# A two-part model kernel on one core: smaller first transfers, gates in column groups, and adaLN weight chunks moved between TensorE, VectorE and the expert stage

## The chip, the cores and the metric

The kernel runs on one core of a Trainium2 chip. The metric is the device time of one execution in microseconds; the median of several runs is compared.

## What is computed

256 tokens of width 1024 in float32 go through two blocks. The first block has two layers, each a mixer, a layer norm and a mixture of experts; the second has two layers with adaLN modulation, two attentions and a feed-forward part. Shortened:

```python
def first_block(x, ...):
    h = x
    for i in range(2):
        mix = gla_mixer(h, ...) if i == 0 else mlstm_mixer(h, ...)
        h = layer_norm(ALPHA * h + mix, ln_g[i, 0], ln_b[i, 0])
        h = layer_norm(ALPHA * h + grouped_moe(h, ...), ln_g[i, 1], ln_b[i, 1])
    return h
# gla_mixer:   x @ w_in (3072 columns, and 16 of low rank for the decay), chunked linear attention, @ w_out
# mlstm_mixer: x @ w_in (4096 columns, and 8 gate columns), causal conv, chunked recurrence, @ w_out
# grouped_moe: 16 experts in 4 groups, best group, best 2 in it; y += gate * ((silu(t@w1) * (t@w3)) @ w2)
# second_block, per layer l: sh1, sc1, gt1, sh2, sc2, gt2 = split(silu(c) @ w_ada[l] + b_ada[l], 6)
#   h = rms(x) * (1 + sc1) + sh1; x += gt1 * (mixed attentions of h @ w_in[l]) @ w_out[l]
#   h = rms(x) * (1 + sc2) + sh2; x += gt2 * relu(h @ w_ff1[l])**2 @ w_ff2[l]
```

## The kernel before

**Stages.** They follow each other on all engines: mixer one (`gla_*`), its expert stage (`moe_*`, l=0), mixer two (`mlstm_*`), its expert stage (l=1), and the two layers of the second block (`dit_*`). Each engine runs its own program; semaphores join them.

**Weights.** All dense weights come in chunks of 1024 x 512 (2 MB) into a ring of four slots in SBUF. In the mixers slots 0 to 2 take the mixer's own chunks in turn, and slot 3 takes adaLN chunks of `w_ada`, 24 in all, that the second block needs much later: whichever engine has room multiplies them with silu(c) beforehand. In the expert stages the four ring slots and two more in the arena hold w1, w3 and w2 of a pair of experts; there are eight pairs. SyncE (SP) issues every load in a fixed order and waits before each until its slot is free (`slot_left`, L344, L404): a load that waits holds back all loads behind it.

**Precision.** A matmul in full precision is made of three products of a high and a low part (`three`, L612). ScalarE casts the high part of a quarter of a chunk (`mix_weight_hi`, L759), VectorE subtracts to get the low part in place (`mix_weight_lo`, L764), TensorE multiplies. Mixer one has 32 such steps n, mixer two 40; ScalarE and VectorE are up to three steps ahead (`LOOK`). Between the products each engine does at a fixed n what else the mixer needs; the tables and the `if n == ...` lines set that order by hand.

**adaLN chunks.** On TensorE a chunk is 16 products of 32 columns (`ada_rows`, L849, a table `*_ADA` says at which n), ScalarE copies (`ada_keep`) and eight small products fold the result (`ada_fold`, L864, table `*_FOLD`). On VectorE it is eight steps over 128x512 (`ada_step`, L711 and L714), summed over the partitions by four small products of TensorE (`ada_tensor`). Before, chunks 0 to 4 go to TensorE in mixer one and 5 to 9 in mixer two; VectorE takes later ones in the second block.

**Around the change.** At the start x is turned (`turn_x`, L792), split into `x_hi`, `x_lo` (L800, L805), the product with the 16 low-rank columns is made (24 products), and then n=0 follows. Mixer two begins with 48 products for the 8 gate columns. In the expert stages TensorE turns and routes (L507, L1354), multiplies constants into an unused bank (`keep_clock`, L785; one filling is one 128x512 product in full precision), waits for VectorE's choice of experts, computes places (L1361 to L1363), gathers tokens (L1399) and goes through the pairs (`up_pair` L1414, `down_pair` L1432). The second block's layers begin with such fillings and the turn of the modulated x (L2313). In mixer two VectorE's `weighed` (L2112) prepares what TensorE's state product (L1825) needs after n=24.

## Time and profile before

| | |
|---|---|
| median of 3 runs | 1673.93 us (1670.14 to 1676.1) |
| the profiled execution's own time | 1675.98 us |
| its span in the profile | 1674.2 us |
| granted TensorE clock, mean | 0.986 |
| TensorE busy | 1590.4 us, 95% |
| VectorE busy | 861.7 us, 51% |
| ScalarE busy | 650.4 us, 39% |
| bytes moved | 425.36 MB, mean 254 GB/s |

Times in the profile count from the span's start. PE is TensorE, DVE VectorE, ACT ScalarE, SP SyncE; "SPq" is a DMA issued by SP. A row of a timeline is: start, duration of the group, engine, line, operation, output<-input, partitions, elements, count, and in brackets the idle time before it with what ended it. L12 is line 12 of the kernel.

### The profile page before, as it was taken

To read this page: it belongs to the slowest core of one execution; us is meant where nothing else is said; L and a number is where in the kernel's file an instruction comes from. 1 tells how busy PE (TensorE), PEld (TensorE's weight loads), DVE (VectorE), ACT (ScalarE), POOL (GpSimd) and SP (SyncE) were. 2 spreads that over 40 slices of the span, in tenths; PEclk is the share of its full clock that TensorE was granted. 3 is DMA by queue.
4 is the path that set the end of the run, shared out by engine and by line. 5 is a ranking of instruction groups with operands and counts; after the bars stand their busy time and mean duration, and the time that the engine had idled before them with its cause. 6 is when DMAs were issued, how large, how long until landed. Compare 5 with 4: busy or idle time off the path is not lost.

```text
span 1674.2 us, 21147 instructions
## 1 busy us (share of the span) xinstructions
PE 1590.4 (95%) x8666; PEld 1089.5 (65%) x8666; DVE 861.7 (51%) x1316; ACT 650.4 (39%) x1056; POOL 41.4 (2%) x67
## 2 busy tenths in 40 slices
PE   5999899998999989999999999999999999999998
PEld 5766443442777654344337776689987777679997
DVE  2656112112766660212148964577777976566555
ACT  3434111111544421111136855544446676544443
POOL 2000000000000000000003000000002000000000
PEclk8999999999999999999999999999999999999999
DMA  9755899999676458999975424568764544537541
GB/s 318 273 187 207 349 427 425 421 426 307 197 222 170 186 214 336 423 426 425 424 276 160 167 101 176 199 253 301 263 249 167 176 153 175 191 113 300 201 152 26
DMA packets 114382, 425.36 MB, mean 254 GB/s; under 512 B 5020, under 2 KB 5368, under 8 KB 101352
## 3 DMA queue, kind: packets, MB, share of 16 engines
q1 hardware_dynamic: 110624, 416.81, 66.1%
q0 software_dynamic: 2304, 6.95, 1.5%
q8 instruction: 72, 1.18, 0.3%
q10 hardware_dynamic: 1352, 0.18, 0.1%
q14 instruction: 30, 0.25, 0.0%
HBM read 421.82 MB, written 1.05 MB: 253 GB/s over the span
## 4 chain that ended last, share of the span: by engine, by line
PE 74%; DVE 10%; ACT 6%; DVEq 4%; issue 2%; DMA 2%; ACTq 0%; SPq 0%
PE bank L612 35%; PE bank L1414 13%; PE bank L1432 7%; PE bank L1399 4%; PE bank L1444 3%; DVEq L713 2%; PE bank L2649 2%; DVE ring_r L2908 2%; DMA ring<-in_gla_w_in 1%; PE bank L785 1%; ACT parts_dit L560 1%; PE bank L849 1%; DVE parts_dit L563 1%; DVE ada_part L714 1%; PE bank L2651 1%
## 5 line engine op out<-in xcount | busy, mean ns | idle before, releaser
L1414 PE MATMUL bank<-ring,arena 128*64 128x512 f32 x1024 | 226.1, 594 | 1.5 <-ACT arena L1508 1.5
L612 PE MATMUL bank<-ring_r,x_hi 128*128 128x512 f32 x528 | 210.2, 398 | 0.0
L1696 DVE TENSOR_TENSOR arena<-arena,bank 128x512 f32<-128x512 f32 x16 | 16.7, 1044 | 363.0 <-PE bank L1414 363.0
L563 DVE TENSOR_TENSOR parts_dit<-ring,parts_dit 128x2048 fp32r<-128x2048 f32 x66 | 151.2, 2291 | 80.9 <-ACT parts_dit L560 80.8
L1414 PEld LDWEIGHTS bank<-ring,arena 128*64 128x64 f32 x1024 | 72.8, 137 | 139.7 <-issue 139.7
L612 PE MATMUL bank<-x_hi,parts_dit 128*128 128x256 f32 x896 | 163.1, 281 | 0.0
L612 PE MATMUL bank<-parts_dit,f_hi 128*128 128x512 f32 x512 | 160.5, 395 | 2.3 <-DVE parts_dit L563 1.4
L560 ACT CAST parts_dit<-ring 128x2048 fp32r<-128x2048 f32 x66 | 125.0, 1897 | 95.5 <-PE bank L612 95.5
L612 PEld LDWEIGHTS bank<-x_hi,parts_dit 128*128 128x128 f32 x896 | 138.5, 188 | 1.9 <-DVE parts_dit L563 1.7
L612 PE MATMUL bank<-in_whi,x_hi 128*128 128x512 f32 x304 | 125.4, 412 | 1.3 <-DVE x_lo L2350 1.3
L1432 PE MATMUL bank<-arena 128*64 128x512 f32 x512 | 115.1, 603 | 10.8 <-ACT arena L1534 10.8
L612 PE MATMUL bank<-x_lo,parts_dit 128*128 128x256 f32 x448 | 125.2, 280 | 0.0
L764 DVE TENSOR_TENSOR ring_r<-ring,mix_whi 128x1024 fp32r<-128x1024 f32 x72 | 86.8, 1221 | 68.0 <-ACT mix_whi L759 67.1
L612 PE MATMUL bank<-in_whi,x_lo 128*128 128x512 f32 x304 | 119.3, 392 | 0.0
L612 PEld LDWEIGHTS bank<-ring_r,x_hi 128*128 128x128 f32 x528 | 99.6, 189 | 19.4 <-issue 0.2
L612 PEld LDWEIGHTS bank<-parts_dit,f_hi 128*128 128x128 f32 x512 | 94.0, 188 | 26.3 <-DVE parts_dit L563 7.1
L2908 DVE TENSOR_TENSOR ring_r<-ring,in_whi 128x1024 fp32r<-128x1024 f32 x76 | 93.5, 1234 | 29.1 <-ACT in_whi L2733 27.7
L759 ACT CAST mix_whi<-ring 128x1024 fp32r<-128x1024 f32 x72 | 74.5, 1046 | 70.7 <-PE bank L612 58.2
L612 PE MATMUL bank<-parts_dit,f_lo 128*128 128x512 f32 x256 | 99.8, 390 | 0.0
L2733 ACT CAST in_whi<-ring 128x1024 fp32r<-128x1024 f32 x76 | 79.7, 1055 | 35.9 <-PE bank L612 35.8
L1432 PEld LDWEIGHTS bank<-arena 128*64 128x64 f32 x512 | 35.7, 138 | 79.9 <-issue 65.2
L612 PEld LDWEIGHTS bank<-x_lo,parts_dit 128*128 128x128 f32 x448 | 84.0, 188 | 0.2
(372 smaller groups left out, 2583.0 us busy)
## 6 DMA issues: line engine op xcount, KB each, us to landing
ring<-in_moe_w SPq DMA_DIRECT2D x64, 2048.0 KB, 12.5
ring<-in_w_ff SPq DMA_DIRECT2D x32, 2048.0 KB, 8.9
arena<-in_moe_w SPq DMA_DIRECT2D x28, 2048.0 KB, 13.0
ring<-in_w_ada SPq DMA_DIRECT2D x24, 2048.0 KB, 8.4
ring<-in_w_in SPq DMA_DIRECT2D x20, 2048.0 KB, 8.8
ring<-in_mlstm_w_in SPq DMA_DIRECT2D x8, 2048.0 KB, 13.8
ring<-in_gla_w_in SPq DMA_DIRECT2D x6, 2048.0 KB, 14.4
arena<-in_moe_w SPq DMA_DIRECT2D x8, 1024.0 KB, 10.7
```

Of the source, the lines that this page charges most:

```text
L560: return nc.scalar.copy(part_view(where, 0, h, form), half_of(ring[:, SLOT_OF[n], :], form, h))
L563: return nc.vector.tensor_tensor(part_view(where, 1, h, form), half_of(ring[:, SLOT_OF[n], :], form, h), part_view(where, 0, h, form).bitc ...
L612: last = pe.matmul(out, a[ka], b[kb], start=(first and i == 0), stop=(final and i == 2))
L713: dve.drain()
L759: nc.scalar.copy(quarter_hi(form, at), quarter_of(ring_slot(NUMBER[name]), form, q)).then_inc(in_hi, 1)
L764: nc.vector.tensor_tensor(quarter_of(ring_slot_r(NUMBER[name]), form, q), quarter_of(ring_slot(NUMBER[name]), form, q), quarter_hi(form, a ...
L1399: last = pe.matmul(ps[c // 4][:, (c % 4) * P:(c % 4 + 1) * P], x_sb[:, tt, c * P:(c + 1) * P], s_pick[:, tt, :], start=(tt == 0), stop=(tt ...
L1414: last = pe.matmul(bank[halves[h], :], s_x[:, p % 2, c, halves[h]], w[h][:, c, :], start=(c == 0), stop=(c == DC - 1))
L1432: last = pe.matmul(ps[6 + m][halves[h], :], s_hid[:, f, halves[h]], w[h][:, f, m * PSB:(m + 1) * PSB], start=(f == 0), stop=(f == 3))
L1444: last = pe.matmul(ps[2 * tt + m][:, :], s_gateT[:, p % 2, tt * P:(tt + 1) * P], s_y[:, m * PSB:(m + 1) * PSB], start=True, stop=True)
L2733: nc.scalar.copy(in_hi_of(l, n), ring_slot(NUMBER["in", l, j])[:, 2 * q:2 * q + 2, :]).then_inc(in_hi, 1)
L2908: v.tensor_tensor(ring_slot_r(NUMBER["in", l, j])[:, c, :], ring_slot(NUMBER["in", l, j])[:, c, :], in_hi_of(l, n).bitcast(F32), ALU.subtr ...
```

## The change

1. **Start.** The first chunk comes as two halves of 256 columns. The constants are laid out anew: 384 columns go right behind it, the other 2528 behind the last input chunk. The Pool queue holds its small loads (router, gates, gains) and the `rows` tables until chunk 3 of mixer one has landed. The low-rank product moves behind n=0.
2. **adaLN chunks.** Chunk 2 (mixer one) and chunks 6, 7, 8 (mixer two) go from TensorE to VectorE, in pieces at given n. Chunks 4 and 9 stay on TensorE but move into the expert stages: rows behind the router's products, fold behind the places.
3. **Fillings.** `keep_clock` in the expert stages 2 to 3 and 4 to 3; in the second block 10 to 6 for layer 0, and 2 new ones for layer 1.
4. **Mixer two.** The gates become 16 products in full precision in four column groups of 32, a copy by ScalarE and two products with a table of ones that sum the groups; copy, sums and the gate rows' activations come after n=0, VectorE's row chain after n=1. ScalarE's second head root (`head_root(1)`) moves behind the sigmoids of n=31, the second half turn from n=32 to 33.

TensorE in the expert stage of mixer two, from the router's sums to the gather (`chosen` is VectorE's choice, `c_act` silu(c)), before:

```order
L1354 MATMUL bank<-kst,arena 128x16 x2
L785 MATMUL bank<-kst 128x512 x4
L1361 MATMUL bank<-chosen,kst 128x32
L1362 MATMUL bank<-chosen,kst 128x16
L1363 MATMUL bank<-chosen,kst 128x32
L1399 MATMUL bank<-arena,x_sb 128x128 x16
```

and now:

```order
L1390 MATMUL bank<-kst,arena 128x16 x2
L875 MATMUL bank<-ring,c_act 32x512 x8
L811 MATMUL bank<-kst 128x512 x3
L1398 MATMUL bank<-chosen,kst 128x32
L1399 MATMUL bank<-chosen,kst 128x16
L1400 MATMUL bank<-chosen,kst 128x32
L890 MATMUL bank<-kst,ada_part 128x1 x4
L1440 MATMUL bank<-arena,x_sb 128x128 x16
```

Sixteen row products and the fold of an adaLN chunk now stand here, and one filling fewer.

SP at the beginning of the program (`kst` are the constants), before:

```order
L3143 DMA kst<-shape_constants 128x136
L3145 DMA x_sb<-in_x 128x1024 x2
L344 DMA ring<-in_gla_w_in 128x8x512 x2
L367 DMA kst<-shape_constants 128x2912
L344 DMA ring<-in_gla_w_in 128x8x512
L344 DMA ring<-in_w_ada 128x8x512
L344 DMA ring<-in_gla_w_in 128x8x512
```

and now, to the first load of an adaLN chunk:

```order
L3202 DMA kst<-shape_constants 128x136
L3204 DMA x_sb<-in_x 128x1024 x2
L348 DMA ring<-in_gla_w_in 128x8x256
L349 DMA ring<-in_gla_w_in 128x8x256
L375 DMA kst<-shape_constants 128x384
L352 DMA ring<-in_gla_w_in 128x8x512 x2
L352 DMA ring<-in_w_ada 128x8x512
```

The first chunk is in two parts, and 2528 columns of constants stand further behind.

VectorE in mixer two from n=22 on (L2098 and L2112 are `decays` and `weighed`, L2128 the state), before:

```order
L2098 SCALAR_TENSOR_TENSOR arena<-bank,arena,kst 128x128 x4
L2103 COPY arena<-bank 128x4
L2105 TENSOR_TENSOR arena<-arena,bank 128x256 x2
L2103 COPY arena<-bank 128x4
L2105 TENSOR_TENSOR arena<-arena,bank 128x256 x2
L764 TENSOR_TENSOR ring_r<-ring,mix_whi 128x1024
L2112 SCALAR_TENSOR_TENSOR arena<-bank,arena 128x512
L2171 TENSOR_TENSOR arena<-arena,rstd 128x2x2
L764 TENSOR_TENSOR ring_r<-ring,mix_whi 128x1024
L2128 COPY arena<-bank 128x257 x2
L2130 SCALAR_TENSOR_TENSOR arena<-arena,bank 128x257 x2
```

and now (L2156, L2170, L2186 are the same three, L723 and L726 the adaLN steps):

```order
L726 SCALAR_TENSOR_TENSOR ada_part<-ring,c_act,ada_part 128x512 x2
L2156 SCALAR_TENSOR_TENSOR arena<-bank,arena,kst 128x128 x4
L2161 COPY arena<-bank 128x4
L2163 TENSOR_TENSOR arena<-arena,bank 128x256 x2
L2161 COPY arena<-bank 128x4
L2163 TENSOR_TENSOR arena<-arena,bank 128x256 x2
L790 TENSOR_TENSOR ring_r<-ring,mix_whi 128x1024
L2170 SCALAR_TENSOR_TENSOR arena<-bank,arena 128x512
L2229 TENSOR_TENSOR arena<-arena,rstd 128x2x2
L790 TENSOR_TENSOR ring_r<-ring,mix_whi 128x1024
L726 SCALAR_TENSOR_TENSOR ada_part<-ring,c_act,ada_part 128x512 x3
L2186 COPY arena<-bank 128x257 x2
```

Two adaLN steps of chunk 8 stand ahead of `decays`, and three behind `weighed`.

```diff
@@ -66,11 +66,12 @@
-    ("ident", P), ("cols", 8), ("keep", P), ("addmask", P), ("dil", TT * 2 * T), ("cos_seq", TT * HD), ("sin_seq", TT * HD),
-    ("cos_ax", TT * HD), ("sin_ax", TT * HD), ("reset", T), ("pick", MH * P), ("before", PER * PER),
+    ("ident", P), ("cols", 8), ("keep", P), ("reset", T), ("addmask", P), ("dil", TT * 2 * T), ("cos_seq", TT * HD), ("sin_seq", TT * HD),
+    ("cos_ax", TT * HD), ("sin_ax", TT * HD), ("pick", MH * P), ("before", PER * PER),
...
+SECOND_N = FIRST_N + P + T
@@ -163,9 +164,9 @@
-        add(("gla_out", j), j == 0)
+        add(("gla_out", j), j == N_OUT - 1)
...
-        add(("ml_in", j), 2 <= p < 7)
+        add(("ml_in", j), p in (2, 3, 4, 6, 7))
@@ -214,7 +215,7 @@
-KEPT = {g: i for i, g in enumerate([*range(10), PAIR["out", 0, 1]])}
+KEPT = {g: i for i, g in enumerate([0, 1, 3, 4, 5, 9, PAIR["out", 0, 1]])}
@@ -341,6 +342,13 @@
+            if n == NUMBER["gla_in", 0]:
...
+                half = width // 2
+                sp.dma_start(slot_view(n, width)[:, 0:c, 0:half], src[:, :, 0:half]).then_inc(e_landed[0], 16)
+                sp.dma_start(slot_view(n, width)[:, 0:c, half:width], src[:, :, half:width]).then_inc(
+                    w_landed[SLOT_OF[n]], 16)
+                return
@@ -363,8 +371,11 @@
-                if j == 1:
-                    sp.dma_start(kst[:, FIRST_N:], const[:, FIRST_N:]).then_inc(const_landed, 16)
+                if j == 0:
+                    sp.dma_start(kst[:, FIRST_N:SECOND_N], const[:, FIRST_N:SECOND_N]).then_inc(const_landed, 16)
+                if j == N_GLA_IN - 1:
+                    sp.wait_ge(const_landed, 16)
+                    sp.dma_start(kst[:, SECOND_N:], const[:, SECOND_N:]).then_inc(const_landed, 16)
@@ -715,6 +727,15 @@
+        def mixer_ada(dve, work):
...
+            g, c0, c1 = work
+            if c0 == 0:
+                landed(dve, ada_chunk(g))
+                dve.wait_ge(ada_cols, g - 1)
+            for c in range(c0, c1):
+                ada_step(dve, g, c, ada_part[:, g % 2, :])
@@ -752,7 +773,12 @@
-            if q == 0:
+            if name == ("gla_in", 0):
+                if q == 0:
+                    act.wait_ge(e_landed[0], 16)
+                if q == QUARTERS // 2:
+                    landed(act, NUMBER[name])
+            elif q == 0:
@@ -893,8 +919,9 @@
-        GLA_ADA = {5: 0, 9: 1, 13: 2, 17: 3, 21: 4}
-        GLA_FOLD = {7: 0, 11: 1, 15: 2, 19: 3, 23: 4}
+        GLA_ADA = {5: 0, 9: 1, 19: 3}
+        GLA_FOLD = {7: 0, 11: 1, 18: 2, 21: 3}
+        GLA_WORK = {12: (2, 0, 1), 13: (2, 1, 4), 14: (2, 4, 5), 15: (2, 5, 6), 16: (2, 6, 8)}
@@ -913,12 +940,14 @@
-            pe.wait_ge(low_split, 1)
...
-            for c in range(DC):
-                last = three(pe, ps[3][0:RANK, 0:T], (wr_hi[:, c, :], wr_lo[:, c, :]), (xh[:, c, :], xl[:, c, :]),
-                             c == 0, c == DC - 1)
-            last.then_inc(gla_mm, 1)
...
+            def low_rank():
+                pe.wait_ge(low_split, 1)
+                for c in range(DC):
+                    last = three(pe, ps[3][0:RANK, 0:T], (wr_hi[:, c, :], wr_lo[:, c, :]), (xh[:, c, :], xl[:, c, :]),
+                                 c == 0, c == DC - 1)
+                last.then_inc(gla_mm, 1)
@@ -1015,6 +1044,7 @@
+                    low_rank()
@@ -1047,7 +1077,7 @@
-                    ada_fold(pe, GLA_FOLD[n], ps[3])
+                    (ada_fold if GLA_FOLD[n] in KEPT else ada_tensor)(pe, GLA_FOLD[n], ps[3])
@@ -1266,6 +1300,8 @@
+                if n in GLA_WORK:
+                    mixer_ada(dve, GLA_WORK[n])
@@ -1342,11 +1378,11 @@
-            pe.wait_ge(const_landed, 16)
+            pe.wait_ge(const_landed, 32)
...
-                    keep_clock(pe, ps[1], 2)
+                    keep_clock(pe, ps[1], 3)
@@ -1354,13 +1390,15 @@
-            keep_clock(pe, ps[2], 4)
+            ada_rows(pe, MOE_ADA[l], ps[3])
+            keep_clock(pe, ps[2], 3)
...
+            ada_fold(pe, MOE_ADA[l], ps[3])
@@ -1385,10 +1423,13 @@
+            pe.wait_ge(ada_read, MOE_ADA[l] + 1)
...
-
+            pe.wait_ge(m_added[l], 4 * NE + 1)
...
+        MOE_ADA = (4, 9)
@@ -1482,8 +1523,10 @@
+            ada_keep(act, MOE_ADA[l], ps[3])
...
+            ada_scalar(act, MOE_ADA[l], ps[3])
@@ -1728,8 +1772,11 @@
-        ML_ADA = {4: 5, 9: 6, 14: 7, 18: 8, 22: 9}
-        ML_FOLD = {6: 5, 11: 6, 16: 7, 20: 8, 24: 9}
+        ML_ADA = {4: 5}
+        ML_FOLD = {6: 5, 14: 6, 20: 7, 26: 8}
+        ML_WORK = {7: (6, 0, 3), 9: (6, 3, 5), 10: (6, 5, 6), 12: (6, 6, 8),
+                   14: (7, 0, 2), 16: (7, 2, 5), 17: (7, 5, 6), 18: (7, 6, 8),
+                   20: (8, 0, 2), 21: (8, 2, 3), 22: (8, 3, 5), 24: (8, 5, 8)}
@@ -1751,14 +1798,21 @@
-            pe.wait_ge(low_split, 2)
...
-            for a in range(2):
-                for c in range(DC):
-                    s = slice(a * MH, (a + 1) * MH)
-                    last = three(pe, ps[3][0:MH, a * T:(a + 1) * T], (wm_hi[:, c, s], wm_lo[:, c, s]), (xh[:, c, :], xl[:, c, :]),
-                                 c == 0, c == DC - 1)
+            for half in range(2):
+                for i, x in enumerate((xh, xl)):
+                    for a in range(4):
+                        c = 4 * half + a
+                        last = pe.matmul(ps[3][32 * a:32 * (a + 1), 0:T], w_mgate[:, c, :], x[:, c, :].bitcast(F32),
+                                         start=(half == 0 and i == 0), stop=(half == 1 and i == 1))
...
+            def sum_gates():
+                pe.wait_ge(ml["gates"], 1)
+                for a in range(2):
+                    last = pe.matmul(ps[3][0:MH, a * T:(a + 1) * T], k("sum4")[:, a * MH:(a + 1) * MH], m_sums, start=True,
+                                     stop=True)
+                last.then_inc(ml["mm"], 1)
@@ -1870,6 +1924,8 @@
+                if n == 0:
+                    sum_gates()
@@ -1931,21 +1987,23 @@
-            act.wait_ge(small_landed, SMALL)
-            nc.scalar.copy(wm_hi[:, :, :], w_mgate[:, :, :]).then_inc(low_hi, 1)
...
-            nc.scalar.activation(m_ig, ps[3][0:MH, 0:T], ACT.Identity, bias=b_mgate[:, 0:1])
-            nc.scalar.activation(m_fz, ps[3][0:MH, T:2 * T], ACT.Identity, bias=b_mgate[:, 1:2]).then_inc(ml["gates"], 1)
-            act.drain()
-            nc.scalar.activation(m_tmp, m_fz, ACT.Abs)
-            act.drain()
-            nc.scalar.activation(m_tmp, m_tmp, ACT.Exp, scale=-1.0)
-            act.drain()
-            nc.scalar.activation(m_tmp, m_tmp, ACT.Ln, bias=kcol(ONE, MH)).then_inc(ml["soft"], 1)
+            nc.scalar.copy(m_sums, ps[3][:, 0:T]).then_inc(ml["gates"], 1)
+            def gate_rows():
+                act.wait_ge(ml["mm"], 2)
+                act.wait_ge(small_landed, SMALL)
+                nc.scalar.activation(m_ig, ps[3][0:MH, 0:T], ACT.Identity, bias=b_mgate[:, 0:1])
+                nc.scalar.activation(m_fz, ps[3][0:MH, T:2 * T], ACT.Identity, bias=b_mgate[:, 1:2]).then_inc(ml["gates"], 1)
+                act.drain()
+                nc.scalar.activation(m_tmp, m_fz, ACT.Abs)
+                act.drain()
+                nc.scalar.activation(m_tmp, m_tmp, ACT.Exp, scale=-1.0)
+                act.drain()
+                nc.scalar.activation(m_tmp, m_tmp, ACT.Ln, bias=kcol(ONE, MH)).then_inc(ml["soft"], 1)
@@ -2042,21 +2100,21 @@
+                if n == 31:
+                    head_root(1)
...
-            dve.wait_ge(low_hi, 2)
...
-            dve.drain()
-            v.tensor_tensor(wm_lo[:, :, :], w_mgate[:, :, :], wm_hi[:, :, :].bitcast(F32), ALU.subtract).then_inc(low_split, 1)
-            for n in range(LOOK):
-                mix_weight_lo(dve, base + n, *ML_STEPS[n], "cols")
+            mix_weight_lo(dve, base, *ML_STEPS[0], "cols")
...
+            for n in range(1, LOOK):
+                mix_weight_lo(dve, base + n, *ML_STEPS[n], "cols")
@@ -2220,14 +2278,16 @@
-                if n == 33:
+                if n == 34:
...
-                if n == 0:
+                if n == 1:
...
+                if n in ML_WORK:
+                    mixer_ada(dve, ML_WORK[n])
@@ -2497,8 +2557,7 @@
-            if l == 0:
-                keep_clock(pe, ps[4], 10)
+            keep_clock(pe, ps[4] if l == 0 else ps[0], 6 if l == 0 else 2)
@@ -3155,6 +3214,7 @@
+            landed(pool, NUMBER["gla_in", 3])
```

## Rows read from the trace of the kernel before

**Rows 1.** The page: busy time of the engines, and shares of the last chain

```profile
PE 1590.4 (95%) x8666; PEld 1089.5 (65%) x8666; DVE 861.7 (51%) x1316; ACT 650.4 (39%) x1056; POOL 41.4 (2%) x67
...
PE 74%; DVE 10%; ACT 6%; DVEq 4%; issue 2%; DMA 2%; ACTq 0%; SPq 0%
```

**Rows 2.** Stretches: length, busy us of PE, PEld, DVE, ACT, POOL, PEclk, DMA share, GB/s

```profile
16.50:30.20 13.70, 4.89 (x23) 4.89 (x24) 4.63 (x4) 4.15 (x5) 0.00 (x0) 0.50 1.04 400
...
225.50:255.20 29.70, 29.02 (x144) 12.46 (x143) 5.22 (x15) 3.61 (x7) 0.00 (x0) 1.00 1.00 424
430.28:435.84 5.56, 5.56 (x48) 4.04 (x49) 0.00 (x0) 0.00 (x0) 0.00 (x0) 1.00 0.67 265
...
463.40:542.20 78.80, 78.80 (x514) 60.05 (x512) 50.23 (x104) 36.08 (x54) 0.00 (x0) 1.00 0.66 193
...
624.50:634.50 10.00, 9.23 (x52) 4.67 (x52) 1.87 (x8) 2.27 (x3) 0.00 (x0) 1.00 0.08 16
...
620.70:624.10 3.40, 3.40 (x19) 3.40 (x18) 0.00 (x0) 0.00 (x0) 0.00 (x0) 0.50 0.63 270
```

**Rows 3.** DMA, 5 to 12 us in 40 slices, and an issue: KB, us to landing

```profile
GB/s 410 421 363 386 413 354 387 375 395 401 433 337 293 179 120 85 85 123 117 111 64 23 26 0 0 0 12 26 47 56 73 76 79 94 91 164 190 220 281 393
...
kst<-shape_constants SPq DMA_DIRECT2D x1, 1456.0 KB, 28.9
```

**Rows 4.** Timeline of the start, TensorE and ScalarE

```profile
5.93 3.65 PE L792 MATMUL bank<-kst,x_sb 128*128 128x128 f32 x16 [5.93 <-DMA x_sb<-in_x]
...
22.96 2.94 ACT L759 CAST mix_whi<-ring 128x1024 fp32r<-128x1024 f32 x3 [12.56 <-DMA ring<-in_gla_w_in]
...
25.31 0.58 PE L612 MATMUL bank<-x_hi,mix_whi 128*128 128x256 f32 x1 [11.16 <-DVE ring_r L764]
...
30.43 0.24 PE L925 MATMUL bank<-kst,arena 92*128 92x92 f32 x1
```

**Rows 5.** Timeline: one instance of each piece that moves (TensorE, VectorE)

```profile
46.96 1.92 PE L849 MATMUL bank<-ring,c_act 128*32 128x512 f32 x16
...
54.58 0.95 PE L864 MATMUL bank<-kst,ada_part 128*128 128x1 f32 x8
...
157.62 0.91 PE L507 MATMUL bank<-arena,w_router 128*32 128x128 f32 x16 [1.26 <-ACT arena L495]
...
1096.59 2.41 DVE L714 SCALAR_TENSOR_TENSOR ada_part<-ring,c_act,ada_part 128x512 f32<-128x512 f32 x3
```

**Rows 6.** Timeline of the first expert stage's beginning, TensorE

```profile
163.43 5.30 PE L785 MATMUL bank<-kst 128*128 128x512 f32 x8
```

**Rows 7.** Mixer two: timeline of VectorE and TensorE; an issue of the page

```profile
537.71 0.68 DVE L2112 SCALAR_TENSOR_TENSOR arena<-bank,arena 128x512 f32<-128x512 f32 x1
...
542.15 1.14 PE L1825 MATMUL bank<-arena 64*128 64x257 f32 x8
...
579.09 0.50 PE L612 MATMUL bank<-mix_whi,x_hi 128*128 128x512 f32 x1 [2.37 <-ACT y_sb L2043]
...
ring<-in_w_ada SPq DMA_DIRECT2D x24, 2048.0 KB, 8.4
```

**Rows 8.** Timeline of the second expert stage's beginning, SP and TensorE

```profile
557.84 0.58 SPq L404 DMA_DIRECT2D ring<-in_moe_w  x1
...
600.13 3.14 SPq L404 DMA_DIRECT2D ring<-in_moe_w  x2
...
612.06 3.68 PE L785 MATMUL bank<-kst 128*128 128x512 f32 x8
...
617.60 0.41 PE L1361 MATMUL bank<-chosen,kst 128*128 128x32 f32 x2 [1.86 <-DVE chosen L1617]
...
626.13 4.08 PE L1414 MATMUL bank<-ring,arena 128*64 128x512 f32 x18 [0.77 <-ACT arena L1508]
```

**Rows 9.** Timeline of the second block's layers' beginnings, TensorE

```profile
865.21 10.55 PE L785 MATMUL bank<-kst 128*128 128x512 f32 x20 [3.38 <-issue]
...
1275.70 1.68 PE L2313 MATMUL bank<-kst,x_sb 128*128 128x128 f32 x8 [2.20 <-DVE x_sb L2436]
```

More of the change, by code:

```diff
@@ L184 @@
 assert len(PAIR) == DEPTH * N_ADA
-assert PAIR["ml_in", ML_ORDER[6]] == 9
+assert PAIR["ml_in", ML_ORDER[7]] == 9
 AFTER_MOE = [NUMBER["ml_in", 0], NUMBER["in", 0, 0]]
@@ L258, in build @@
         w_router = sb("w_router", [P, DC, 32])
-        w_mgate = sb("w_mgate", [P, DC, 2 * MH])
+        w_mgate = sb("w_mgate", [P, DC, 32])
         b_mgate = sb("b_mgate", [MH, 2])
@@ L384, in e_arrived @@
         def e_arrived(eng, k, count):
-            eng.wait_ge(e_landed[k], 16 * count)
+            eng.wait_ge(e_landed[k], 16 * (count + (1 if k == 0 else 0)))
         def moe_sync(sp, l):
@@ L451, in build @@
             (w_router[:, :, 0:NE], A["router_w"].rearrange("(p c) n -> p c n", p=P)),
-            (w_mgate[:, :, :], by_rows(A["mlstm_w_in"][0], PSB * N_ML_IN, 2 * MH)),
+            (w_mgate[:, :, 0:2 * MH], by_rows(A["mlstm_w_in"][0], PSB * N_ML_IN, 2 * MH)),
         ]
@@ L1068, in gla_scalar @@
                 turned_hi(act, 0, b, b, 4 + b)
-            act.wait_ge(w_rank_landed, 16)
-            nc.scalar.copy(wr_hi[:, :, :], w_rank[:, :, :]).then_inc(low_hi, 1)
             for n in range(LOOK):
                 mix_weight_hi(act, n, *GLA_STEPS[n], "cols")
+                if n == 0:
+                    act.wait_ge(w_rank_landed, 16)
+                    nc.scalar.copy(wr_hi[:, :, :], w_rank[:, :, :]).then_inc(low_hi, 1)
             act.wait_ge(gla_mm, 1)
@@ L1159, in gla_vector @@
             v.memset(w_router[:, :, NE:32], 0.0)
+            v.memset(w_mgate[:, :, 2 * MH:32], 0.0)
             for b in range(4):
                 turned_lo(dve, 0, b, b, 4 + b)
-            dve.wait_ge(low_hi, 1)
-            v.tensor_tensor(wr_lo[:, :, :], w_rank[:, :, :], wr_hi[:, :, :].bitcast(F32), ALU.subtract).then_inc(low_split, 1)
             for n in range(LOOK):
                 mix_weight_lo(dve, n, *GLA_STEPS[n], "cols")
+                if n == 0:
+                    dve.wait_ge(low_hi, 1)
+                    v.tensor_tensor(wr_lo[:, :, :], w_rank[:, :, :], wr_hi[:, :, :].bitcast(F32), ALU.subtract).then_inc(
+                        low_split, 1)
             def cumulate():
@@ L1563, in moe_vector @@
             v.memset(place[:, :, :], 0.0)
+            dve.wait_ge(const_landed, 32)
             dve.wait_ge(rt_exp, l + 1)
@@ L1717, in build @@
         m_ig, m_fz, m_tmp, m_bc, m_a, m_r, m_wk, m_wi = (area(42.5 + j, T, parts=MH) for j in range(8))
-        wm_hi, wm_lo = (area_r(n, a, [DC, 2 * MH]) for n, a in (("wm_hi", 51), ("wm_lo", 51.5)))
+        m_sums = area(54, T)
         m_pack = area(53, T, parts=MH)
@@ L1872, in mlstm_tensor @@
                 last.then_inc(in_used, 1)
+                if n == 0:
+                    sum_gates()
                 if n == 6:
@@ L1910, in mlstm_tensor @@
                     turn_half(0)
-                if n == 32:
+                if n == 33:
                     turn_half(1)
                 if n == 4:
-                    pe.wait_ge(ml["gates"], 1)
+                    pe.wait_ge(ml["gates"], 2)
                 if n in ML_ADA:
@@ L1917, in mlstm_tensor @@
                 if n in ML_FOLD:
-                    ada_fold(pe, ML_FOLD[n], ps[3])
+                    (ada_fold if ML_FOLD[n] in KEPT else ada_tensor)(pe, ML_FOLD[n], ps[3])
             pe.wait_ge(xt_split, 4 * SPLIT_TURNS[4] + 4)
@@ L1992, in mlstm_scalar @@
                 mix_weight_hi(act, base + ahead, *ML_STEPS[ahead], ml_form(ahead // QUARTERS))
+                if n == 0:
+                    gate_rows()
                 if n == 3:
@@ L2016, in mlstm_scalar @@
                         turned_hi(act, 4, i, b, 4 + i)
-                if n == 31:
-                    head_root(1)
-                if n == 33:
+                if n == 34:
                     for i, b in enumerate(HALVES[1]):
@@ L2222, in mlstm_vector @@
                     gated(1)
-                if n == 33:
+                if n == 34:
                     for i, b in enumerate(HALVES[1]):
@@ L2274, in build @@
         OWN, OWN_OUT, OWN_FF = 3, 1, 2
-        READ_ADA = [(10, N_ADA), (8, 10)]
+        READ_ADA = [(9, N_ADA), (8, 10)]
         ATT_STEPS = {11: (0, 0, 1), 12: (0, 1, 2), 13: (0, 2, 3), 15: (0, 3, 5), 17: (0, 5, 6), 19: (0, 6, 8)}
```

## The prediction

> **What bounds the kernel now.** The page comes first: TensorE is busy 95% of the span and the chain of work that ended last is 74% TensorE [rows 1]. So an instruction taken off TensorE is worth its own duration wherever TensorE runs without a gap, and the rest of the question is where it has gaps. The table of stretches [rows 2] shows both kinds. Inside the expert stage a pair of experts takes 29.70 us, TensorE busy 29.02, while the DMA runs at 424 GB/s with share 1.00: two limits at once. In mixer two, 463.4 to 542.2, TensorE has no gap, VectorE is busy 50.23 of 78.80, the DMA two thirds. The column PEclk shows where TensorE's clock was granted at half (0.50, that is 1.2 instead of 2.4 GHz): 16.5 to 30.2, and at 620.7 for 3.4 us, each time after TensorE had idled. 3.4 us of busy TensorE at half level cost 1.7 us. The timelines [rows 3 to 9] then give each place its price. The bound below which a measurement of this kernel cannot tell a change from none is 0.3%, 5 us.
>
> **The start: +11.2 us.** TensorE's first product of the mixer starts at 25.31, after 11.16 us of idling; behind it stands ScalarE's first cast, 12.56 us idle for the DMA of the first chunk [rows 4]. The bytes were not there because the queues nearly stood from about 7.5 to 10.5 us (slices 15 to 32 of the 40 that part 5 to 12 us; before them about 400 GB/s [rows 3]), while the small weights of the Pool queue were on the way; after that the `rows` tables and 1456 KB of constants, which took 28.9 us to land [rows 3], shared the rate with it. The change sends the first chunk as two halves, 1 MB each, directly behind x, and all of that small traffic later. x's first tile is there at 5.93 [rows 4] and its second, 512 KB behind it, by 6.8 to 7.2; 1 MB at about 390 GB/s is 2.7 us: the half lands at 9.6 to 10. From a landing to the first product it takes 25.31 − 22.96 = 2.35 us [rows 4], so the product starts at 12.0 to 12.4 (x's turn ends at 9.58 [rows 4], its casts are done before). n=0 is 24 products of 256 columns; 48 of them take 5.56 at full clock [rows 2], so 2.8: it ends at 15.3. The rank product, 24 such, 2.8 us, now stands behind it: 18.1. Before, n=0 ended at 30.43 [rows 4]: gain 12.3, less 1.7 if one stretch at half clock remains, which I expect about half the time: 11.2. Low end 0: the halves land no earlier. High end 12.5.
>
> **Mixer one: +3.7.** Chunks 2 and 4 lose their 16 row products, 1.92 us each in the row, 1.85 net of the overlap of ends [rows 5]: 3.7. Chunk 2's eight VectorE steps (2.41 us for three [rows 5], 0.8 each) fall where VectorE is idle over half the time. The fold of chunk 4, 0.8 [rows 5], goes too, but at n=24 TensorE then arrives as much earlier at a wait for ScalarE: nothing.
>
> **MoE0: +0.5.** As the order of the second expert stage shows (the first is the same), rows and three fillings stand where four fillings stood. The four took 5.30 us and the next product followed directly [rows 6]; three fillings (0.92 each at full clock: 3.68 for four [rows 8]) and the rows are 1.85 + 2.76 = 4.6. VectorE's choice ends the wait either way. A clock drop less may give 0.9; the fold costs 0.8: −0.7 to +1.2, taken 0.5.
>
> **Mixer two: +10.** The 48 gate products take 5.56 us [rows 2]. Now there are 16 full-precision ones in four column groups: the router's 16 of that kind, 128 columns wide, take 0.91 [rows 5]; twice as wide 1.82; the two products that sum the groups fill the array alone: at the groups' price 0.23, at four times that, which I take because the four groups no longer run side by side, 0.9. Gain 2.9. Chunks 6 to 9 lose their row products: 4 × 1.85 = 7.4. One fold fewer: 0.8. The wait of 2.37 us for ScalarE's sigmoid at n=31 [rows 7] goes, since the head's root stands behind it now: 2.4. Gross 13.5. Against it: 24 steps on VectorE, 24 × 0.82 = 19.7 us, onto 50 busy us [rows 2] of a stretch that becomes about 71. That is nearly full, so its short queues will be late. The place that I can price is the state product after n=24, 542.15; VectorE's weighing for it ended at 538.39 [rows 7], 3.8 us ahead. Rows 9 gone brings TensorE 1.9 nearer; five steps (n=20 to 22) ahead of it delay VectorE by 4.1: 2.2 us of waiting. The same kind costs about 0.5 at n=5 and 0.7 at the next state: 3.4 in all. Net 10.0. Ends: 13.5 (VectorE keeps pace) and 8 (VectorE also waits for chunks 7 and 8: it now releases their slot itself, a landing takes 8.4 us [rows 7], and it stands about 3 us at n=20).
>
> The Trainium skill, "VectorE: DVE Perf Modes", section "The DRAIN you can't avoid", says that an operation is followed by a drain of its duration less 266 ns; by that a step would be 0.75 + 0.48 = 1.23 us and the state's wait 2 us longer. The same section lets an operation that is not held start earlier, and the row bears that out: three steps in 2.41. A rival below.
>
> **MoE1: −5.0.** SP issues the loads in a fixed order and waits in it. Before: slot 3 at 557.84, then slot 1, then slots 2 and 0 at 600.13 [rows 8]. Chunk 9 now sits in slot 3 until its row products inside MoE1, behind the router's: 612.06 + 1.85 = 613.9. SP waits for it with slots 2 and 0 queued behind, though both are free at 600.13; slot 0 is half of the first pair. Then slots 3, 2, 0 come one after another at 424 GB/s, 4.94 us each: 615.3 + 14.8 = 630.1, against the first product of the pair at 626.13 [rows 8]. 4.0 to 4.5 late, an idle spell and the half clock behind it about 2, but the half-clock stretch at 620.7 [rows 2], costing 1.6 in the gather, follows the wait of 1.86 for `chosen` [rows 8], and three fillings and the rows cover that: −5.0. The DMA regains the rest: it stood at 16 GB/s from 624.5 to 634.5 [rows 2] and this room takes the two late arena loads. Ends: −3 and −14 (every late microsecond of 600 to 614 stays, because a pair has only 29.70 − 29.67 spare of the DMA, 12.58 MB at 424 GB/s).
>
> The Trainium skill, "DMA: Bandwidth & Descriptors", section "Specifications", names about 358 GB/s as the share of one core; by it three chunks take 17.6 instead of 14.8 us and this term would be −7.8. This trace disagrees with 424 over 29.7 us [rows 2], so the sum keeps to it.
>
> **The last two layers: +3.9.** Layer 0 runs ten fillings, 10.55 us, and the turn stands behind them [rows 9]. Six are gone by 872.0; VectorE's second tile is the next limit at about 872.5: +3.2 (2.7 to 3.4). In layer 1 two fillings lie inside the 2.20 us wait at 1275.70 [rows 9] and may spare a half-clock stretch behind it, worth 1.7 like the one at 620.7, or nothing: 0.7.
>
> **Sum.** 11.2 + 3.7 + 0.5 + 10.0 − 5.0 + 3.9 = 24.3. The profiled execution took 1675.98: 1651.7. The median of the runs is 2.05 lower; so 1650.
>
> **Rivals.**
> (A) VectorE keeps pace and MoE1 costs only 3: +3.5 and +2, up to 8 with a start of 12.5: 1644. For: 19.7 us fit in 28.5 idle. Against: queues are late locally, not on average.
> (B) The loads of MoE1 stay late for the stage, 14 instead of 5: 1659. For: the DMA's share of 1.00. Against: the slots wait about 10 us between landing and use there.
> (C) The first half does not land early, because x's own bytes or the split into packets of half the length take the rate: 1661. For: only that no row shows such a load; against: 400 GB/s before 8 us [rows 3].
> (D) Steps on VectorE cost 1.23: mixer two gains 7 to 8: 1653.
> (E) The other side. New short waits of TensorE in mixer two, n=5 to 26, drop its clock to half again and again. Each drop in the trace followed an idle spell; there is none now in that stretch [rows 2], and the change puts VectorE's lateness there. At half clock a microsecond of work takes two, so once more than 24.3 × 2 = 49 us of the 71 run at 1.2 GHz the kernel is slower; all of it would give 1650 + 35 = 1685. Against: at 620.7 the full clock was back after 3.4 us of busy TensorE, and the waits that I price are single ones of 0.5 to 2.2 us.
>
> **Chances.** Forecast 0.58; A 0.17; B 0.09; C 0.05; D 0.05; B and C together, or half the sum for reasons not seen, 0.03 (about 1670, no difference); E 0.03. Faster by over 0.3%: 0.94; within 0.3%: 0.03; slower: 0.03. The range goes from A with its best ends, 1640, to C, 1661.
>
> **What would show it.** First product near 12.2 and n=0 over by 15.5; the start wrong if ScalarE's first cast still waits for the DMA beyond 12. Mixer two: VectorE over 65 us busy between the same steps, TensorE's waits for weighing near 2 us. MoE1: TensorE idle 4 to 5 us ahead of the first pair, waiting for the load of slot 0; if it does not wait, that step is wrong. Layer 0: 6 fillings, then the turn at 3 us less. The forecast fails as a whole if new waits of TensorE for VectorE in mixer two sum to more than 7 us.

## The result and the profile after

The changed kernel took 1660.02 us (1659.31 to 1661.92, four runs), the kernel before 1673.06 beside it (1670.14 to 1676.1): ratio 0.9924, 95% interval 0.9903 to 0.9944. That is 13.0 us less, inside the range, 10 above the forecast of 1650, and only 1 below the range's upper end. That end was set by rival C, which did not happen: that the time still fell inside is partly luck. The profiled execution after took 1659.87, the one before 1675.98: between the two traces lie 16.1, and 3 of them are only that the profiled execution before lay high among its runs. The sum of 24.3 is to be held against 16.1.

"Before" and "after" stand below for the two kernels' traces. The waits of TensorE show most of it at a glance (us in total, times, longest). The view of after:

```profile
PE bank L811 <- issue: 10.0, 3, 5.1
...
PE bank L1455 <- DMA ring<-in_moe_w: 5.4, 1, 5.4
...
PE bank L624 <- DVE ring_r L790: 3.8, 2, 3.4
...
PE bank L624 <- ACT arena L2093: 1.7, 1, 1.7
...
PE bank L1879 <- DVE arena L2170: 0.8, 1, 0.8
...
PE bank L875 <- DMA ring<-in_w_ada: 0.7, 1, 0.7
```

The wait of 11.16 for the first chunk's low part [rows 4] is now 3.40, the sigmoid's 2.37 [rows 7] is gone, and one of 5.40 for expert weights is new.

The timeline of TensorE in after, at the points that answer to [rows 4, 7, 8, 9]:

```profile
12.95 0.55 PE L624 MATMUL bank<-x_hi,mix_whi 128*128 128x256 f32 x1 [3.40 <-DVE ring_r L790]
...
20.88 0.24 PE L954 MATMUL bank<-kst,arena 92*128 92x92 f32 x1
...
417.97 0.64 PE L1806 MATMUL bank<-x_hi,w_mgate 128*32 128x256 f32 x8 [1.88 <-DVE x_lo L831]
...
519.49 0.50 PE L624 MATMUL bank<-mix_whi,x_hi 128*128 128x512 f32 x1 [1.74 <-ACT arena L2093]
...
521.97 1.14 PE L1879 MATMUL bank<-arena 64*128 64x257 f32 x8 [0.82 <-DVE arena L2170]
...
593.14 0.41 PE L1398 MATMUL bank<-chosen,kst 128*128 128x32 f32 x2 [0.78 <-DVE chosen L1661]
...
607.75 4.79 PE L1455 MATMUL bank<-ring,arena 128*64 128x512 f32 x12 [5.40 <-DMA ring<-in_moe_w]
...
848.80 5.42 PE L811 MATMUL bank<-kst 128*128 128x512 f32 x12 [3.39 <-issue]
...
1059.19 1.94 PE L2373 MATMUL bank<-kst,x_sb 128*128 128x128 f32 x8 [2.83 <-DVE x_sb L2496]
```

Subtracting the start of the same instruction in the two traces gives a ledger. The forecast beside it is the prediction's term.

| up to | before | after | gained so far | in this stretch | forecast |
|---|---|---|---|---|---|
| first work behind n=0 and the rank product | 30.43 | 20.88 | 9.55 | 9.6 | 11.2 |
| router, first expert stage | 157.62 | 144.90 | 12.72 | 3.2 | 3.7 |
| last pair, first expert stage | 402.62 | 388.43 | 14.19 | 1.5 | 0.5 |
| gates, mixer two | 430.28 | 417.97 | 12.31 | −1.9 | none |
| router, second expert stage | 607.13 | 582.66 | 24.47 | 12.2 | 10.0 |
| first pair, second expert stage | 626.13 | 607.75 | 18.38 | −6.1 | −5.0 with the next |
| last pair, second expert stage | 851.11 | 834.69 | 16.42 | −2.0 | |
| layer 0, first mixer product | 880.56 | 861.08 | 19.48 | 3.1 | 3.2 |
| end | 1674.2 | 1658.1 | 16.1 | −3.4 | 0.7 |

Where the clock was at half in after (length, busy us of PE, PEld, DVE, ACT, POOL, PEclk, DMA share, GB/s):

```profile
12.95:18.06 5.11, 5.11 (x24) 5.09 (x25) 2.42 (x3) 1.04 (x1) 0.00 (x0) 1.00 1.05 386
147.80:154.60 6.80, 6.71 (x41) 2.53 (x40) 4.84 (x16) 1.23 (x4) 2.31 (x1) 0.51 0.69 280
404.00:410.80 6.80, 6.56 (x8) 2.74 (x9) 5.16 (x7) 2.51 (x3) 1.06 (x2) 0.53 1.00 204
594.90:601.70 6.80, 5.94 (x28) 5.94 (x29) 1.37 (x8) 0.00 (x0) 0.00 (x0) 0.51 1.00 425
605.00:611.60 6.60, 3.85 (x10) 1.24 (x12) 0.00 (x0) 0.00 (x0) 0.00 (x0) 0.50 1.00 427
943.10:946.50 3.40, 3.40 (x12) 2.78 (x11) 1.31 (x2) 1.19 (x3) 0.00 (x0) 0.53 0.02 5
1059.20:1062.50 3.30, 3.30 (x12) 2.98 (x13) 0.00 (x0) 2.12 (x7) 0.00 (x0) 0.52 0.00 0
```

In the second expert stage two stretches stand where one of 3.40 stood [rows 2]. The last two rows are new, and the same work ran at full clock before. A stretch of 3.4 us at 857.6 is left out here; before has one at the same work. In the first row the clock's column says 1.00, yet 24 products took 5.11 us, 0.21 each, as at half; in this trace the column does not show that stretch at the very start, the spacing of the products does (a second trace of the same kernel has it in the column too, from 13.2 on).

### The profile page after: what moved, and what is told of

Its sections match the earlier page's. It is cut to its first block, busy times and chain, and to the rows that moved or that the text cites. A ratio compares the mean times of both kernels' runs of the same rounds, so it can differ in the third digit from the quotient of the medians.

```text
span 1658.1 us, 21045 instructions
## 1 busy us (share of the span) xinstructions
PE 1581.1 (95%) x8586; PEld 1085.3 (65%) x8586; DVE 885.5 (53%) x1348; ACT 647.0 (39%) x1051; POOL 40.4 (2%) x67
## 4 chain that ended last, share of the span: by engine, by line
PE 72%; DVE 12%; ACT 6%; DVEq 5%; DMA 4%; issue 2%; ACTq 0%; SPq 0%
PE bank L624 34%; PE bank L1455 14%; PE bank L1473 7%; PE bank L1440 3%; PE bank L1485 3%; DVEq L725 2%; DVE ring_r L2967 2%; PE bank L2708 2%; DMA ring<-in_w_ada 1%; DVE ada_part L726 1%; DMA ring<-in_moe_w 1%; ACT parts_dit L572 1%; DVE parts_dit L575 1%; PE bank L811 1%; DMA ring<-in_w_ff 1%
## 6 DMA issues: line engine op xcount, KB each, us to landing
ring<-in_moe_w SPq DMA_DIRECT2D x64, 2048.0 KB, 13.3
```

## The experiments

Each ran beside the kernel before; ratios are to it. The changed kernel's ratio is 0.9924.

### The order of SP's loads in the second expert stage

```diff
-by_release = sorted(range(SLOTS), key=lambda k: last[k]) + list(range(SLOTS, ROLES))
+by_release = [k for k in sorted(range(SLOTS), key=lambda k: last[k]) if k != SLOTS - 1] + list(range(SLOTS - 1, ROLES))
```

> The changed kernel with one difference: in the second expert stage SP asks for slots 1, 2 and 0 first and for slot 3 (the one that chunk 9 holds) after them. Theory (SP's order made TensorE wait 5.40 us ahead of the first pair, and the idle spell brought a second half-clock stretch worth about 2): no wait for a DMA of the expert weights at the first pair, it starts about 5.4 us earlier in the stage, 1653 to 1654 in all against 1660. Rival (the DMA's rate is the bound at this place, whatever the order): the wait only moves to slot 3 a few products later, and the time stays at 1658 to 1660.

1655.17 us (1651.44 to 1657.29), ratio 0.9874 (0.9846 to 0.9902). In after, the view of SP's waits has this row:

```profile
SPq L416 <- PE bank L875: 33.8, 1, 33.8
```

SP stood 33.8 us until the row products of chunk 9 had freed slot 3, with loads for free slots queued behind. With the order turned, TensorE at the same place:

```profile
595.89 5.46 PE L1440 MATMUL bank<-arena,x_sb 128*128 128x128 f32 x32 [0.90 <-DVE arena L1592]
602.12 4.08 PE L1455 MATMUL bank<-ring,arena 128*64 128x512 f32 x18 [0.77 <-ACT arena L1551]
```

No wait for weights is left. Counted from the router's first product, the same instructions come 0.7 us earlier than in after in the gather, 5.8 at the first pair and 7.5 four products later: 6.8 us from this place alone, 5.4 of waiting and the rest the half-clock stretch behind it. The medians differ by less, 4.9 us, and the time lies 1 to 2 above the theory's 1653 to 1654. The mechanism holds; the rival, that the DMA's rate is the bound there whatever the order, falls.

### The Pool queue's wait alone

```diff
 pool.dma_start(w_up, A["gla_w_gate_up"][0]).then_inc(w_up_landed, 16)
+landed(pool, NUMBER["gla_in", 3])
```

> The kernel before with one line of the change: the Pool queue holds its small loads and the rows tables until chunk 3 of mixer one has landed. The first chunk stays whole, the constants stay where they were. Theory (the small Pool loads stalled the queues and the rows tables shared them): the first product of the mixer starts at about 15 instead of 25.31, so this line alone brings 9 to 10 of the start's gain, 1663 to 1665. Rival (halving the chunk is what brings it): the first product stays later than 20, the time within 4 us of before.

1668.76 us (1664.39 to 1671.41), ratio 0.9949 (0.9923 to 0.9976). ScalarE's first cast, in this kernel:

```profile
13.03 2.94 ACT L759 CAST mix_whi<-ring 128x1024 fp32r<-128x1024 f32 x3 [2.64 <-DMA ring<-in_gla_w_in]
```

It was 22.96 [rows 4]. n=0 was over at 18.50, 11.9 us earlier than before, and 2.4 earlier than in the changed kernel. So this line brings all of the start's gain and more, at that point. Of the 11.9 only 7.6 were left by 85 us, when TensorE had waited for the second adaLN chunk and run a stretch at half clock:

```profile
68.79 2.06 PE L849 MATMUL bank<-ring,c_act 128*32 128x512 f32 x12 [2.64 <-DMA ring<-in_w_ada]
```

In the changed kernel TensorE waits 0.7 for such a chunk. The theory on the cause of the stall holds; its 9 to 10 us at the end do not, 4.6 are left between the spans and 6.0 between the medians.

### The first chunk whole

```diff
-sp.dma_start(slot_view(n, width)[:, 0:c, 0:half], src[:, :, 0:half]).then_inc(e_landed[0], 16)
-sp.dma_start(slot_view(n, width)[:, 0:c, half:width], src[:, :, half:width]).then_inc(
-    w_landed[SLOT_OF[n]], 16)
-return
```

> The changed kernel with the first chunk in one piece, everything else as changed. Theory: the chunk lands 2.7 to 3 us later than its first half did, the first product of the mixer at 15.7 instead of 12.95, 2.7 to 3 us slower, 1662 to 1663. Rival (the later traffic sets the pace of mixer one, not the first product): the same time as the changed kernel, 1659 to 1661.

1658.67 us (1656.86 to 1661.27), ratio 0.9906 (0.9877 to 0.9935). The first product came 2.2 us later than in after, at 15.17, and at 52 us the lag was 1.5 (2.1 against the second trace of the changed kernel, below). The medians do not show it: 1.5 us faster than the changed kernel beside it, within what the runs differ. So the theory's 2.7 to 3 us at the end failed, and the rival's "the same time" held: halving the chunk is worth 1.5 to 2.1 us at 52 us by the traces, and nothing that the medians can tell.

### The low-rank product ahead of n=0 again

```diff
+low_rank()
...
                 if n == 0:
-                    low_rank()
                     turn_params()
```

(and the casts of its weights ahead of the first steps on ScalarE and VectorE)

> The changed kernel with the low-rank product back ahead of n=0 (on ScalarE, VectorE and TensorE), everything else as changed. In the changed kernel TensorE idles 3.40 us ahead of n=0 and n=0 then takes 5.1 us, its products 0.21 apart; with the Pool wait alone the low-rank product filled that idle time, n=0 took 2.8 us and was over at 18.5 instead of 18.1 with the rank product already done. Theory (the reordering gave away the cover): rank product 11.2 to 14.0, n=0 over at 16.8 to 17.2 instead of 20.88 for both, 3.5 to 4 us faster, 1656 to 1657. Rival (n=0 runs at half pace in any order, because the engine has been idle before it): over at 19 to 19.3, 1.7 faster at most.

1656.61 us (1655.56 to 1658.66), ratio 0.9901 (0.9873 to 0.9929); the changed kernel beside it 1660.13 (below). TensorE:

```profile
11.01 0.28 PE L624 MATMUL bank<-x_hi,wr_hi 128*16 128x256 f32 x1 [1.69 <-DVE wr_lo L1195]
...
16.65 0.25 PE L956 MATMUL bank<-kst,arena 92*128 92x92 f32 x1
```

Both products, low-rank and n=0, are done at 16.65 instead of 20.88; the idle time of 3.40 is filled. The time is 3.5 us less by the medians, and by the spans 4.2 less than after and 5.1 less than the changed kernel's second trace. The reordering in the change cost that much.

### The changed kernel again

> The changed kernel itself once more, on the chip that runs the others of this call. Theory: 1659 to 1662, the waits of its first profile at the same places. What may differ is where the stretches at half clock and the waits behind code loads fall (so far 1.48 us in mixer two's fillings).

1660.13 us (1658.58 to 1661.06), ratio 0.9916 (0.9888 to 0.9944). Between its two traces the lag of the same instruction swings from −3.1 to +3.1 us: the half-clock stretch at the first expert stage's beginning lay elsewhere, and the entry to mixer two came 2.4 us later in the second. So a term under some 2 us cannot be read off the end of two traces.

The second trace also shows what sets the first pair of the second expert stage. Here the gather ran at full clock:

```profile
598.83 3.84 PE L1440 MATMUL bank<-arena,x_sb 128*128 128x128 f32 x32 [0.90 <-DVE arena L1592]
610.59 1.98 PE L1455 MATMUL bank<-ring,arena 128*64 128x512 f32 x4 [7.92 <-DMA ring<-in_moe_w]
```

The wait grew from 5.40 to 7.92, and the pair began 24.9 us after the router's first product, against 25.1 in after. The landing sets this time; a faster or slower gather ahead of it changes nothing.

### Both edits

> The changed kernel with both edits: SP's order in the second expert stage with slot 3 last, and the low-rank product ahead of n=0. Theory: the gains add, 5 to 7 and 3.5 to 4, 1649 to 1652. Rival: the start's gain is taken back by waits for chunks within mixer one, 1653 to 1655.

> The kernel with both edits (slot 3 last in SP's order, low-rank product ahead of n=0) once more, as the base of the two that follow. Theory: 1648 to 1651.

SP's order and the low-rank product first: 1649.27 us (1643.91 to 1654.18), ratio 0.9855 (0.9816 to 0.9893), and again 1651.07 (1649.47 to 1652.28), 0.9851 (0.9832 to 0.9871). The gains add: this beats both kernels.

### Fewer fillings at the beginning of mixer two

```diff
-            keep_clock(pe, ps[4], 6)
+            keep_clock(pe, ps[4], 2)
```

> The changed kernel with 2 instead of 6 fillings at the beginning of mixer two. The trace of the changed kernel has x ready on VectorE at 408.08, but the turn starts at 414.18, behind 12 passes of fillings of which 7 ran at half clock, and a gap of 1.48 us. Theory (the fillings are the bound there): the turn starts at 408 to 410, 4 to 5 us earlier, 1655 to 1656. Rival (without the fillings the clock stays at half through the turn and the gates, or VectorE's splitting is the bound): 1658 to 1661.

1659.93 us (1657.08 to 1664.38), ratio 0.9893 (0.9864 to 0.9922). By the median nothing was gained; the ratio is a little lower than the changed kernel's, but the intervals overlap. TensorE in this kernel (a filling is two records, so "x4" is two fillings):

```profile
406.61 3.78 PE L811 MATMUL bank<-kst 128*128 128x512 f32 x4 [6.75 <-issue]
410.18 1.70 PE L818 MATMUL bank<-kst,x_sb 128*128 128x128 f32 x7
416.56 2.08 PE L818 MATMUL bank<-kst,x_sb 128*128 128x128 f32 x9 [4.68 <-issue]
```

The turn did start four us earlier, and then stopped in the middle for 4.68 us, waiting for nothing that a semaphore shows. A packet of the instruction queue falls in that gap (DMA view, 413.5 to 415.5):

```profile
q8 instruction: 1, 0.02, 2.9%
```

It carries 16 KB, starts at 414.16, and TensorE goes on at 416.56, 2.4 us later. The same pair stands in each trace: packet and restart at 401.81 and 404.24, 411.49 and 413.75 in after, 417.19 and 419.62 in before. The second gap also keeps its place in TensorE's program: it lies ahead of the 1972nd product (counted in the trace) in ten of the twelve traces of changed kernels, be that a filling (after) or a part of the turn (here); with the whole first chunk it is the 1973rd, and one trace has no such gap. I read the packet as a load of TensorE's code, and the fillings as work that hides it; no run changed the load itself, so this stays a reading. Neither theory nor rival had the gap. The rival was right in its other half: the clock was at half again from 415.2 to 425.5, through the turn's end and the gates, which took 3.6 us instead of 1.9, and its 1658 to 1661 holds.

### Chunks 6 to 8 back on TensorE

```diff
-        ML_ADA = {4: 5}
-        ML_FOLD = {6: 5, 14: 6, 20: 7, 26: 8}
+        ML_ADA = {4: 5, 9: 6, 14: 7, 20: 8}
+        ML_FOLD = {6: 5, 11: 6, 16: 7, 22: 8}
```

(and `ML_WORK` empty)

> The changed kernel with chunks 6, 7 and 8 back on TensorE in mixer two (rows at n=9, 14, 20, folds at n=11, 16, 22), and no adaLN steps of VectorE there. Theory: TensorE gets 3 x 1.85 = 5.6 us more work and loses the waits that VectorE's fuller list caused (0.44, 1.74, 0.82 and 0.20 us): about 2.4 us slower than the changed kernel, 1662 to 1663. Rival (VectorE's list costs nothing net, the waits stay): 5 to 6 slower, 1665 to 1666. Rival (moving them was no gain): 1660 or less.

> The kernel with both edits, and chunks 6, 7, 8 back on TensorE in mixer two. The first kernel of this kind was 2.0 us slower inside mixer two plus one stretch at half clock, but stalls at the beginning of mixer two blurred its whole time. Theory: 2 to 2.5 us slower than the base at the end of mixer two by the two traces, 1651 to 1653 in all. Rival: 5.6 or more slower.

On the changed kernel: 1665.38 us (1658.58 to 1672.34, nine runs), ratio 0.9938 (0.9915 to 0.996). Its runs lie far apart. The trace shows 2.7 us lost between the first expert stage's last pair and mixer two's gates, where the second gap named "issue" is 4.14 instead of 1.48. On the kernel with both edits: 1655.30 us (1651.59 to 1657.33), ratio 0.9874 (0.9851 to 0.9898), 4.2 slower than its base, where 2 to 2.5 had been expected. VectorE and TensorE between 420 and 520 us, in the changed kernel and in the first of these two:

```profile
420.00:520.00 100.00, 97.82 (x668) 82.61 (x669) 82.43 (x162) 52.62 (x87) 0.00 (x0) 1.00 0.58 171
```

```profile
420.00:520.00 100.00, 97.90 (x711) 78.52 (x710) 67.97 (x130) 50.95 (x84) 0.00 (x0) 1.00 0.67 192
```

The steps put 14 us more on VectorE in this window and save TensorE its row products; the waits that they cause (1.74 and 0.82 in after) are gone here, while the 0.44 at n=5 stays (0.45): that one is not theirs. From the gates to the router the two kernels take 4.5 and 5.1 us longer than after and the base; 1.7 of each is a half-clock stretch near 520 us. Moving the three chunks is worth about 4 us, between my 2.4 and the rival's 5.6 or more.

### Row products in place of the first fillings

```diff
-                    keep_clock(pe, ps[1], 3)
+                    ada_rows(pe, MOE_ADA[l], ps[1])
...
-            ada_rows(pe, MOE_ADA[l], ps[3])
-            keep_clock(pe, ps[2], 3)
+            keep_clock(pe, ps[2], 4)
```

> The kernel with both edits, and in both expert stages the row products of chunks 4 and 9 take the place of the first three fillings, behind the first tile's turn, with four fillings instead of three at the second place. Theory: there they cover a wait for ScalarE and VectorE, as the fillings did; behind the router's products they stand ahead of fillings and in a half-clock stretch. Slot 3 is free about 6 us earlier. Per stage 0.5 to 1.5 us faster: 1647 to 1648. Rival (VectorE's choice is what ends that place, the order of TensorE's work ahead of it changes nothing): same as the base.

1651.86 us (1649.29 to 1652.47), ratio 0.9855 (0.9835 to 0.9875): as its base, 1651.07. The rival held.

### The fillings of the last two layers as before

```diff
-            keep_clock(pe, ps[4] if l == 0 else ps[0], 6 if l == 0 else 2)
+            if l == 0:
+                keep_clock(pe, ps[4], 10)
```

> The changed kernel with the fillings of the second block as before: ten ahead of layer 0's turn, none in layer 1. Theory (the fillings stood on the path in layer 0): the turn of layer 0 and the first product of its mixer 3 us later than in the changed kernel; what of it remains at the end depends on where the half-clock stretches at 943 and 1059 fall: 1660 to 1663. Rival (the shorter filling is what caused those two stretches, which the kernel before did not have): they are gone, and the time is the same or lower, 1659 to 1660.

1662.39 us (1659.14 to 1665.47), ratio 0.992 (0.9895 to 0.9944). Against after, layer 0's first mixer product lost 3.1 us at this place, and the half-clock stretches near 946 and 1062 were there again. So they do not come from the shorter filling; what brings them stays open. They were missing in before and in the kernel with the whole chunk, which has the changed kernel's fillings, and the changed kernel's second trace has only the later one. In layer 1, where this kernel has no fillings, the wait of 2.20 is back, and yet no half-clock stretch follows it. So the two fillings there are not shown to be what spares the stretch that before has at 1276.

## Why the prediction was right and where it was wrong

**Direction and range held**, and four of the six terms lie within 2 us. The sum was 8.2 us too high against the trace; the last two layers (4.2 us), the second expert stage (3.1) and the start (1.6) make it up, and the first expert stage gave 1.0 more than forecast.

**The start, 11.2 forecast, 9.6 measured.** The cause was right: the small loads of the Pool queue held up the first chunk, and their wait, together with that of the `rows` tables behind them, brings n=0 to 18.50; the two are not separated. The landing was nearly right (first product at 12.95, forecast 12.0 to 12.4). The term has a slip: 12.3 less half of 1.7 is 11.45, not 11.2. The stretch at half clock, to which I gave a chance of one half, came, and cost 2.3 instead of 1.7: all but the last two of n=0's products ran at that pace, 5.1 us as in before. I took the moved low-rank product as neutral; it had filled the idle time, and putting it back gave 3.5 us. That part of the change works against the rest.

**Mixer one and first expert stage, 3.7 and 0.5 forecast, 3.2 and 1.5 measured.** At n=24 the wait for ScalarE grew from 0.44 to 1.34, as the term has it; a new wait of 0.69 for a weight chunk at 52 us is the rest. Up to the first pair the expert stage lost 0.2, inside my ends; 1.7 came from a half-clock stretch at 197 us that before had and after has not. That gain is luck.

**Mixer two, 10.0 forecast, 10.3 measured** from the first expert stage's last pair to the router, but of other parts. Inside the mixer 12.2 were gained. The gates' term holds: 1.9 us and 1.0 for the two sums, forecast 1.8 and 0.9, against 5.7 before; no run tests it or the sigmoid's wait alone. Waits of 0.44, 1.74, 0.82 and 0.20, 3.2 in all, stand against my 3.4, and the 0.44 is not due to the steps. VectorE was busy 63.0 us over the mixer's same products where before it was 50.2; I had asked for over 65. At the entry 1.9 were lost, a step that the sum did not have: nearly all of the half-clock stretch of 6.8 us fell on the fillings, where half of before's fell into its idle gap, and a second gap of 1.48 came on top. The 12.2 hold 1.7 from a half-clock stretch at 580 that is gone: together they nearly cancel, so 10.3 meets 10.0 by some luck.

By the drain rule of the Trainium skill, "VectorE: DVE Perf Modes", section "The DRAIN you can't avoid", the wait ahead of the state product would have been the 2.2 us of the sum and 2 more. It was 0.82, and with the 1.74 just ahead of it 2.6; three steps in a row took 2.40 us in after's mixer two, as the row of before has it (2.41). The trace does not bear that rival out for these steps.

**Second expert stage, −5.0 forecast, −8.1 measured.** The mechanism was right: SP waits for slot 3, TensorE for the pair, 5.40 us. The row products ended as forecast, and the 2 us of half clock behind the pair came. Two steps failed in size. The first pair began 6.1 us late, where I had 4.0 to 4.5: I gave the three loads 16.2 us from the end of the row products, and they landed 8.0, 13.3 and 18.2 us after it; the first took longer, the others came 5 us apart as forecast. And I took 1.6 back because fillings and rows would cover the clock's drop in the gather. They did not cover it (the clock fell at 594.7, between a wait of 0.78 and one of 0.90, for 6.8 us instead of 3.4), but that was no loss either: the pair waits for a landing, so nothing could be had back ahead of it. The −7.8 that the prediction works out from a slower DMA comes nearer by chance only: the rate was 425 and 427 GB/s. Rival B, 14 us, fell, though its 1659 is nearly the time: behind the first pair nothing more was lost beyond the 2.0 at half clock.

**The last two layers, +3.9 forecast, −0.3 measured.** This term missed by most, 4.2 us. The shorter filling brought 3.1 of my 3.2. Then 3.4 were lost: two new stretches at half clock, 1.7 each less what layer 1 gained (the stretch at 1276 is gone, as forecast, but not shown to be so by the fillings, as said above), and a wait of 2.83 instead of 1.62 for x in layer 0's end, behind a weight chunk that took 14.0 us to land instead of 12.8. No term stood for these, and what brings the stretches stays open.

**The median.** I carried the 2.05 us between profiled execution and median of before over to after. After's profiled execution lies at its median, so that offset came from the one execution and not from the kernel.

Rival A fell in both halves, and rival C with the first product at 12.95. Rival E found nothing in the changed kernel: in both its traces the granted clock was 1.00 from the gates to the router, with all the new waits. Four other kernels with the same steps (SP's order, both edits in one of two traces, fewer fillings, fillings as before) have one half-clock stretch of 3.4 us that starts between 511 and 525, and so have both kernels without the steps (525.4 and 519.6): it costs 1.7 us and is not bound to those waits.

## What to carry to other kernels

A step that is free by its own engine's timeline can sit in the middle of a queue that it does not use: ask what SP, which waits in order, will hold back while it waits for the buffer. Put the one late buffer last in the order of loads, not where it falls by its number. Before moving work away from the front of an idle time, look whether it is what fills it; and compare two traces instruction by instruction before believing a term under 2 us. What is saved ahead of a wait for a landing is not saved: do not credit it against the wait.

## What was not expected of the hardware

- TensorE's gaps that the profile calls "issue" at the entry to mixer two (6.29 us before, 5.09 and 1.48 after, 6.75 and 4.68 with two fillings) end 2.2 to 2.5 us after the start of a 16 KB packet of the instruction queue. In the changed kernels the second packet follows 7.2 to 10.9 us after the first, with twelve products of fillings between (9.7 in after) as with four (10.0). With the ring's loads under way the DMA was at share 1.00 in after from 404.0 to 410.8.
- The 24 products of n=0 took 5.1 us behind an idle time of 3.40 us (4.4 in the second trace), and 2.8 directly behind the low-rank product. Of the kernels with the halved chunk, both products were over between 16.5 and 18.2 in the five traces with the low-rank product first, and between 19.8 and 20.9 in six with n=0 first. In two of the five the low-rank product itself began at half pace, and those two ended last, at 18.1 and 18.2.
- The same kernel's two traces differ in their half-clock stretches: the changed kernel's second expert stage has two of 6.8 us in one and one of 6.8 in the other, and layer 0 has one of 3.4 near 943 in only one of them. 3.4 us at half clock cost 1.7 where TensorE was busy throughout.
